# A hybrid decoder trunk: the rows of all experts but the last item are combined on GpSimd, those of the last on TensorE

## The chip, the core and the metric

The kernel runs on one core of a Trainium2 chip. The metric is the device time of one execution in microseconds (us); lower is better. In a core, TensorE (PE) multiplies matrices, VectorE (DVE) and ScalarE (ACT) work elementwise, GpSimd (POOL) works elementwise too and issues the indirect (row by row) transfers, and SyncE (SP) issues transfers. They run at the same time and wait for each other only through semaphores. SBUF is the memory that they work in, PSUM the one that TensorE writes its products to.

## The reference

Two residual layers over 512 tokens of width 1024. Each has a token mixer and then a channel mixer, dense in layer 0 and a mixture of 8 experts in layer 1, of which every token uses two. The trunk ends in an RMS norm. The change concerns only the end of the mixture of experts:

```python
top_logit, top_e = lax.top_k(logits, TOP_K)            # TOP_K = 2
gates = jax.nn.softmax(top_logit, axis=-1)
...                                                    # tokens sorted by expert, in blocks of ROW_BLOCK = 128 rows
def expert_block(args):
    xb, e = args
    return (jax.nn.silu(xb @ w1[e]) * (xb @ w3[e])) @ w2[e]
y_rows = lax.map(expert_block, (x_rows, block_e)).reshape(n_rows, d)
y = jax.ops.segment_sum(y_rows.astype(F32) * row_gate[:, None], row_tok, num_segments=n + 1)[:n]
...
h = h + moe_swiglu(...)
return rms_norm(h, final_norm_g)
```

So every token gets two rows, each from one of its experts and scaled by its gate, added to `h`, and then the final norm.

## The kernel before

All arithmetic is float32. A product on TensorE takes its operands in two parts: `hi`, the operand rounded to a shorter format (a copy on ScalarE), and `lo`, the rest (`raw - hi`, a subtraction on VectorE), and a sum of three products (`mm3`, L582 to L585).

The mixture of experts runs as a loop over work items. An item is an expert's block of 128 rows (L1930 and others, `item_one`), or 128 + up to 32 rows at once in a turned form (`item_turned`). In this run there are eight items; the last is of the form `item_one`. An item takes its expert's weights in 7 chunks of 6 pieces, each 128 x 2048 numbers. A piece is loaded by SyncE, rounded by ScalarE in two halves (`round_ahead`, L1189 and L1191) and its rest is formed by VectorE in two halves (`rest_ahead`, L1774 and L1777: two operands, both in SBUF). The pieces run ahead of TensorE in a ring of six. In a chunk of `item_one`, VectorE does, in this order: pieces 8 and 9, `turned` (L1868), pieces 10 and 11, `hidden` (L1863), pieces 12 and 13, and two additions to `yacc` (L1884). TensorE waits for `turned` before it starts the down product, and for a piece's rest before it uses the piece. At the end of an item VectorE has more to do: rests of two pieces that belong to the next item (for the last item to no one), the rows of the next item (L1879), and the last additions to `yacc`.

`yacc` holds the item's output rows. GpSimd runs the loop beside them (L552 to L565): it clears `yacc` and `yturned`, copies a column of row indices (L545, `gather`), gathers the token rows of the next item to `xg` (L548), waits until the item is complete (`item_out`), stores `yacc` to `y_rows` in HBM (L562, L563), and waits for the store to land. TensorE turns the gathered rows near the end of the item (`turn_rows`, L881), also in the last item, where nobody needs them.

After the loop, GpSimd gathers for each of the four tiles of 128 tokens the first and the second expert's row of every token from `y_rows` (L573, eight gathers of 128 rows of 4 KB), and VectorE adds them, scaled by the gates, to `h` (`combine`, L2018, eight). Between them stands the final norm: a square and sum on ScalarE (L1045), the variance on VectorE (L1342), the root on ScalarE (L1047), its reciprocal (L1347) and the product of `h`, the reciprocal and the gain (L1361). SyncE stores each tile (L487).

The order on each engine is written out by hand: an engine does its instructions in the order of the program, and a wait holds up all behind it.

## Time and profile before

| | |
|---|---|
| time, median of 3 runs | 2075.96 us (2074.44 to 2076.59) |
| the profiled execution | 2074.16 us, of which the profile's span is 2072.5 us |
| PE busy | 1995.7 us, 96% |
| DVE busy | 1576.3 us, 76% |
| ACT busy | 1104.1 us, 53% |
| POOL busy | 89.5 us, 4% |
| DMA | 450.97 MB, mean 218 GB/s |

The busy shares are means over the whole span. By slices of a fortieth of the span, VectorE is at six to nine tenths in the items and TensorE at nine, until the last slice and a half, where TensorE has nothing to do. GpSimd's busy time is in short groups, one at each item's start. Times in the rows are in us from the span's start; a duration in a timeline is that of one instruction or of several merged ones (x2).

### The profile page before, as it was taken

The numbers are of one execution on the slowest core, as the hardware profiler recorded it, in microseconds if no ns is written. First come the engines' busy times: TensorE is split into PE (matmuls) and PEld (weight loads), VectorE is DVE, ScalarE is ACT, GpSimd is POOL, SyncE is SP. The second block draws the span as 40 slices with busy tenths as digits, with TensorE's granted clock in tenths as the row PEclk, the third lists the DMA queues.
The fourth block names the chain that finished last, engine by engine and source line by source line (L and its number), as shares of the span: only waits on it lengthen the run. The fifth ranks groups of instructions, "written<-read, shape, count | busy, mean of one in ns | idle before, by whom it ended". The sixth has DMA issues, their size and how long they took to land.

```text
span 2072.5 us, 34371 instructions
## 1 busy us (share of the span) xinstructions
PE 1995.7 (96%) x12246; PEld 1770.0 (85%) x12247; DVE 1576.3 (76%) x1964; ACT 1104.1 (53%) x1269; POOL 89.5 (4%) x104
## 2 busy tenths in 40 slices
PE   7999999999999999999999999999999999999993
PEld 6889787877778788999999988888999888999882
DVE  6866535344468677888888899998888998888996
ACT  6532423323345423555555577777555776555773
POOL 0000000000000002100100010101000101000101
PEclk9999999999999999999999999999999999999997
DMA  5312723132312215777777699999777999776983
GB/s 195 105 59 92 265 80 119 64 121 63 119 61 92 71 52 170 250 261 259 250 252 260 231 378 368 364 379 340 270 243 244 340 378 325 254 259 235 375 318 144
DMA packets 218811, 450.97 MB, mean 218 GB/s; under 512 B 13088, under 2 KB 64304, under 8 KB 218768
## 3 DMA queue, kind: packets, MB, share of 16 engines
q1 hardware_dynamic: 210416, 421.05, 58.2%
q0 software_dynamic: 8352, 29.33, 3.8%
q8 instruction: 29, 0.48, 0.1%
q14 instruction: 14, 0.11, 0.0%
HBM read 432.50 MB, written 17.84 MB: 217 GB/s over the span
## 4 chain that ended last, share of the span: by engine, by line
PE 83%; DVE 10%; issue 3%; ACT 2%; DMA 1%; DVEq 0%; POOL 0%; ACTq 0%; SPq 0%; POOLq 0%
PE ps L583 17%; PE ps L585 17%; PE ps L584 17%; PE ps L925 12%; PE ps L942 8%; PE ps L927 5%; PE ps L944 3%; DVE w_lo L1777 2%; DVE w_lo L1774 1%; PE ps L652 1%; ACT w_hi L1189 1%; DVE w_lo L1331 1%; PE ps L607 1%; PE ps L846 1%; DVE ex L1356 0%
## 5 line engine op out<-in xcount | busy, mean ns | idle before, releaser
L1774 DVE TENSOR_TENSOR w_lo<-raw,w_hi 128x1024 fp32r<-128x1024 f32 x340 | 414.5, 1219 | 81.9 <-ACT w_hi L1189 79.5
L925 PE MATMUL ps<-xt,w_hi 128*128 128x320 f32 x1792 | 465.3, 347 | 2.2 <-DVE xt L1788 1.9
L927 PE MATMUL ps<-xt,w_lo 128*128 128x160 f32 x1792 | 424.2, 237 | 0.0
L1189 ACT ACTIVATE w_hi<-raw 128x1024 fp32r<-128x1024 f32 x340 | 357.4, 1051 | 112.6 <-PE ps L927 61.2
L1777 DVE TENSOR_TENSOR w_lo<-raw,w_hi 128x1024 fp32r<-128x1024 f32 x340 | 414.1, 1218 | 0.0
L1191 ACT ACTIVATE w_hi<-raw 128x1024 fp32r<-128x1024 f32 x340 | 356.4, 1048 | 0.0
L927 PEld LDWEIGHTS ps<-xt,w_lo 128*128 128x128 f32 x1792 | 343.1, 191 | 0.1
L925 PEld LDWEIGHTS ps<-xt,w_hi 128*128 128x128 f32 x1792 | 337.2, 188 | 2.8 <-issue 2.7
L583 PE MATMUL ps<-act_hi,w_hi 128*128 128x512 f32 x608 | 242.1, 398 | 5.2 <-DVE act_lo L1375 5.2
L585 PE MATMUL ps<-act_hi,w_lo 128*128 128x512 f32 x608 | 239.9, 395 | 0.0
L584 PE MATMUL ps<-act_lo,w_hi 128*128 128x512 f32 x608 | 239.9, 395 | 0.0
L942 PE MATMUL ps<-ht,w_hi 128*128 128x320 f32 x896 | 234.0, 346 | 3.5 <-DVE gated L1897 3.5
L944 PE MATMUL ps<-ht,w_lo 128*128 128x160 f32 x896 | 212.3, 237 | 0.0
L583 PE MATMUL ps<-w_hi,xt 128*128 128x512 f32 x448 | 177.7, 397 | 0.7 <-issue 0.7
L585 PE MATMUL ps<-w_hi,xt 128*128 128x512 f32 x448 | 177.9, 397 | 0.0
L584 PE MATMUL ps<-w_lo,xt 128*128 128x512 f32 x448 | 177.1, 395 | 0.0
L942 PEld LDWEIGHTS ps<-ht,w_hi 128*128 128x128 f32 x896 | 168.1, 188 | 4.4 <-DVE gated L1897 4.2
L944 PEld LDWEIGHTS ps<-ht,w_lo 128*128 128x128 f32 x896 | 171.1, 191 | 0.0
L1696 DVE TENSOR_TENSOR hid_d<-silu_d,ps 128x512 f32<-128x512 f32 x22 | 15.1, 688 | 173.0 <-PE ps L585 173.0
L583 PEld LDWEIGHTS ps<-act_hi,w_hi 128*128 128x128 f32 x608 | 114.4, 188 | 34.3 <-issue 3.9
L585 PEld LDWEIGHTS ps<-act_hi,w_lo 128*128 128x128 f32 x608 | 114.4, 188 | 27.1
L584 PEld LDWEIGHTS ps<-act_lo,w_hi 128*128 128x128 f32 x608 | 114.4, 188 | 26.9 <-issue 0.5
(330 smaller groups left out, 3174.7 us busy)
## 6 DMA issues: line engine op xcount, KB each, us to landing
raw<-in_moe_w_dram SPq DMA_DIRECT2D x672, 512.0 KB, 5.4
raw<-in_w_in_dram SPq DMA_DIRECT2D x19, 1024.0 KB, 5.1
raw<-in_ffn_w_gate_dram SPq DMA_DIRECT2D x11, 1024.0 KB, 5.3
raw<-in_ffn_w_up_dram SPq DMA_DIRECT2D x11, 1024.0 KB, 5.4
raw<-in_ffn_w_down_dram SPq DMA_DIRECT2D x11, 1024.0 KB, 4.9
raw<-in_w_out_dram SPq DMA_DIRECT2D x8, 1024.0 KB, 5.0
y_rows<-mult POOLq DMA_DIRECT2D x1, 8192.0 KB, 29.5
y_rows<-yacc POOLq DMA_DIRECT2D x8, 512.0 KB, 5.5
```

The source lines that it names most:

```text
L583: pe.matmul(o_, lhi, rhi, start=start, stop=False)
L584: pe.matmul(o_, lhi, rlo, start=False, stop=False)
L585: return pe.matmul(o_, llo, rhi, start=False, stop=stop)
L607: last = pe.transpose(ps[:, k, i * P:(i + 1) * P], rows_of(m, i)[:, k * P:(k + 1) * P], idt[:, :])
L925: pe.matmul(pairs_of(ps[:, bank, 0:2 * NW]), hi_[:, k % 4, f * P:(f + 1) * P], xt[:, k, :, 0:NW], start=k == 0, stop=False)
L927: last = pe.matmul(ps[:, bank, NW:2 * NW], lo_[:, k % 4, f * P:(f + 1) * P], xt[:, k, 0, 0:NW], start=False, stop=k == KT - 1)
L942: pe.matmul(pairs_of(ps[:, bank, 0:2 * NW]), hi_[:, f % 2, d * P:(d + 1) * P], ht_n[:, f, :, :], start=f == 0, stop=False)
L944: last = pe.matmul(ps[:, bank, NW:2 * NW], lo_[:, f % 2, d * P:(d + 1) * P], ht_n[:, f, 0, :], start=False, stop=f == 3)
L1189: act.activation(slot_hi[p % 6][:, 0:half], raw6(p)[:, 0:half], ACT.Copy).then_inc(w_hi_half, 1)
L1191: act.activation(slot_hi[p % 6][:, half:PIECE], raw6(p)[:, half:PIECE], ACT.Copy).then_inc(w_hi_done, 1)
L1774: dve.tensor_tensor(slot_lo[p % 6][:, 0:half], raw6(p)[:, 0:half], f32(slot_hi[p % 6][:, 0:half]), ALU.subtract)
L1777: dve.tensor_tensor(slot_lo[p % 6][:, half:PIECE], raw6(p)[:, half:PIECE], f32(slot_hi[p % 6][:, half:PIECE]), ALU.subtract).then_inc(w_lo ...
```

## The change

The last item is taken out of GpSimd's loop. Beside it GpSimd no longer gathers rows for a next item. It gathers the rows of all other items from `y_rows` (the last item's rows are zero there), tile by tile, into `xg`, scales them by the gates (a multiplication by one number for each row) and adds them to `h` (eight of each, 128 x 1024). Then it builds `chosen`, a 0/1 matrix of rows by tokens, from the row indices and a list of the token numbers, and loads the gain of the norm. The last item's rows aren't stored. ScalarE and VectorE split `yacc` into `hi` and `lo` when it is complete, and TensorE multiplies them with `chosen`: 8 products with 512 columns for each tile of tokens, of which four have the 32 rows of the item's second part. VectorE adds the product to `h`, scaled by `g_last`, each token's gate for the last item (seven small instructions ahead of the items). A row that holds no token now has the index 512, that of an added row of zeros in `hn_rows`. TensorE's transposes of `xg` in the last item are as before; they now wait until GpSimd is through, by the two small transfers at its end. A root on ScalarE ahead of the norm loads its table.

```diff
@@ -196,12 +196,16 @@
         w_lo2 = sb("w_lo2", [P, 3, PIECE], F32R)
-        comb = [at(f"comb{i}", [P, D], F32, mix0 + i * 4096) for i in range(8)]
         yacc = sb("yacc", [P, 2, D])
+        xg0 = base[0]
         xg = [sb(f"xg{i}", [P, D]) for i in range(2)]
...
         yturned = sb("yturned", [P, KT, NW])
-        growf = yturned.rearrange("p k n -> p (k n)")[:, 0:D]
+        assert 2 * T <= D
+        chosen = at("chosen", [P, 2, T], F32R, xg0)
+        growf = xg[1]
+        last_hi = [w_his[:, b, 0:D] for b in range(2)]
+        last_lo = [w_los[:, b, 0:D] for b in range(2)]
...
@@ -224,7 +230,7 @@
-        hn_dram = nc.dram_tensor("hn_rows", (T, D), F32, kind="Internal").ap()
+        hn_dram = nc.dram_tensor("hn_rows", (T + 1, D), F32, kind="Internal").ap()
         y_dram = nc.dram_tensor("y_rows", ((MAX_BLOCKS + 1) * P, D), F32, kind="Internal").ap()
@@ -509,6 +524,7 @@
                 .then_inc(y_zeroed, 16)
+            pool.dma_start(hn_dram[T:T + 1, :], mult[0:1].rearrange("p c t -> p (c t)")).then_inc(y_zeroed, 16)
             pool.wait_ge(rows_done, 8)
...
@@ -549,7 +565,7 @@
-            with pool.Fori(0, n_items) as n:
+            with pool.Fori(0, n_items - 1) as n:
                 pool.memset(yacc[:, :, :], 0.0).then_inc(yacc_free, 1)
@@ -564,17 +580,42 @@
-            pool.wait_ge(w_lo_done, n_items * IP + (MOE0 + AHEAD))
+            pool.memset(yacc[:, :, :], 0.0).then_inc(yacc_free, 1)
+            pool.memset(yturned[:, :, :], 0.0).then_inc(yacc_free, 1)
+            block = pool.value_load(items[0:1, bass.ds(n_items + 15, 1)], min_val=0, max_val=MAX_BLOCKS - 1)
+            pool.dma_start(token_at[:, :], token_row.partition_broadcast(P)).then_inc(token_rows, 16)
             for b in range(2):
-                pool.wait_ge(xg_loaded[b], n_items * 16)
+                pool.tensor_copy(colf[:, b:b + 1], idx[:, bass.ds(block + b, 1)]).then_inc(chosen_ready, 1)
+            pool.wait_ge(chosen_ready, 2)
+            pool.wait_ge(token_rows, 16)
+            pool.wait_ge(xt_tr, n_items * 2)
+            pool.wait_ge(gates_final, 1)
             pool.nop(nofuse=True)
...
                 for j in range(2):
-                    pool.indirect_dma_start(comb[2 * i + j][:, :], None, y_dram,
+                    if i:
+                        pool.wait_ge(early_added, 2 * (i - 1) + j + 1)
+                        pool.nop(nofuse=True)
+                    pool.indirect_dma_start(xg[j][:, :], None, y_dram,
                                             bass.IndirectOffsetOnAxis(ap=slots[:, i, j:j + 1], axis=0)) \
                         .then_inc(comb_loaded[2 * i + j], 16)
-                if i == 0:
-                    pool.dma_start(growf[:, :], norm_rows[4].partition_broadcast(P)).then_inc(gain_loaded, 16)
+                for j in range(2):
+                    pool.wait_ge(comb_loaded[2 * i + j], 16)
+                    if j:
+                        pool.wait_ge(early_added, 2 * i + 1)
+                    pool.tensor_scalar(xg[j][:, :], xg[j][:, :], rt[:, 12, 4 * j + i:4 * j + i + 1], None, ALU.mult) \
+                        .then_inc(early_scaled, 1)
+                    pool.wait_ge(early_scaled, 2 * i + j + 1)
+                    pool.tensor_tensor(h[:, i, :], xg[j][:, :], h[:, i, :], ALU.add).then_inc(early_added, 1)
+            pool.wait_ge(early_added, 2 * NT)
+            for b in range(2):
+                pool.tensor_scalar(chosen[:, b, :], token_at[:, :], colf[:, b:b + 1], None, ALU.is_equal) \
+                    .then_inc(chosen_ready, 1)
+            pool.dma_start(growf[:, :], norm_rows[4].partition_broadcast(P)).then_inc(gain_loaded, 16)
+            pool.wait_ge(gain_loaded, 16)
+            pool.wait_ge(chosen_ready, 4)
+            for b in range(2):
+                pool.dma_start(token_at[0:1, b * 8:b * 8 + 8], token_row[:, 0:8]).then_inc(xg_loaded[b], 16)
@@ -1009,6 +1050,26 @@
+            pe.wait_ge(chosen_ready, 4)
+            pe.wait_ge(tail_ready, 1)
+            for i in range(NT):
+                to = slice(i * P, (i + 1) * P)
+                for half in range(2):
+                    s_ = slice(half * 512, (half + 1) * 512)
+                    if i == 0:
+                        pe.wait_ge(last_lo_done, half + 1)
+                    pe.matmul(ps[:, 2 * i + half, :], chosen[:, 0, to], last_hi[0][:, s_], start=True, stop=False)
+                    pe.matmul(ps[:, 2 * i + half, :], chosen[:, 0, to], last_lo[0][:, s_], start=False, stop=False)
+                for half in range(2):
+                    s_ = slice(half * 512, (half + 1) * 512)
+                    if i == 0 and half == 0:
+                        pe.wait_ge(last_lo_done, 3)
+                    pe.matmul(ps[:, 2 * i + half, :], chosen[0:TAIL, 1, to], last_hi[1][0:TAIL, s_],
+                              start=False, stop=False)
+                    last = pe.matmul(ps[:, 2 * i + half, :], chosen[0:TAIL, 1, to], last_lo[1][0:TAIL, s_],
+                                     start=False, stop=True)
+                last.then_inc(spread_done, 1)
+
@@ -1313,6 +1374,12 @@
+            act.wait_ge(tail_ready, 1)
+            for half in range(2):
+                s_ = slice(half * 512, (half + 1) * 512)
+                act.activation(last_hi[0][:, s_], yacc[:, 0, s_], ACT.Copy).then_inc(last_hi_done, 1)
+            act.activation(last_hi[1][0:TAIL, :], yacc[0:TAIL, 1, :], ACT.Copy).then_inc(last_hi_done, 1)
+            act.activation(var[:, 0:1], var[:, 0:1], ACT.Sqrt)
             norm(4)
@@ -1857,6 +1924,15 @@
             link(dve.tensor_tensor(g2, rt[:, 9, 4:8], g1, ALU.mult))
+            starts, last_start, in_last = rt[:, 15, 8:16], rt[:, 15, 16:17], rt[:, 15, 20:24]
+            g_last = rt[:, 12, 16:20]
+            link(dve.scalar_tensor_tensor(starts, blocks, 0.0, first_block, ALU.is_gt, ALU.mult))
+            link(dve.tensor_reduce(last_start, starts, AX.X, ALU.max))
+            link(dve.tensor_scalar(last_start, last_start, float(P), None, ALU.mult))
+            link(dve.tensor_scalar(in_last, rt[:, 16, 0:4], last_start, None, ALU.is_ge))
+            link(dve.tensor_tensor(g_last, g1, g2, ALU.subtract))
+            link(dve.tensor_tensor(g_last, g_last, in_last, ALU.mult))
+            dve.tensor_tensor(g_last, g_last, g2, ALU.add).then_inc(gates_final, 1)
@@ -2013,28 +2089,33 @@
-            def combine(i, j):
-                dve.wait_ge(comb_loaded[2 * i + j], 16)
-                ins = dve.scalar_tensor_tensor(h[:, i, :], comb[2 * i + j][:, :], (g1, g2)[j][:, i:i + 1], h[:, i, :],
-                                               ALU.mult, ALU.add)
-                if j:
-                    ins.then_inc(h_ready, 1)
-                else:
-                    link(ins)
-
-            for i in range(NT + 1):
-                if i < NT:
-                    combine(i, 0)
-                if i:
-                    norm_var(4, i - 1)
-                if i < NT:
-                    combine(i, 1)
-                if i:
-                    norm_row(4, i - 1)
+            dve.wait_ge(item_out, n_items * 4 + 4)
+            dve.sem_inc(tail_ready, 1)
+            for half in range(2):
+                s_ = slice(half * 512, (half + 1) * 512)
+                dve.wait_ge(last_hi_done, half + 1)
+                dve.tensor_tensor(last_lo[0][:, s_], yacc[:, 0, s_], f32(last_hi[0][:, s_]), ALU.subtract) \
+                    .then_inc(last_lo_done, 1)
+            dve.wait_ge(last_hi_done, 3)
+            dve.tensor_tensor(last_lo[1][0:TAIL, :], yacc[0:TAIL, 1, :], f32(last_hi[1][0:TAIL, :]), ALU.subtract) \
+                .then_inc(last_lo_done, 1)
+            dve.wait_ge(early_added, 2 * NT)
+
+            def spread(i):
+                dve.wait_ge(spread_done, i + 1)
+                dve.scalar_tensor_tensor(h[:, i, :], ps[:, 2 * i:2 * i + 2, :].rearrange("p a d -> p (a d)"),
+                                         g_last[:, i:i + 1], h[:, i, :], ALU.mult, ALU.add).then_inc(h_ready, 1)
+
+            spread(0)
+            for i in range(NT):
+                if i < NT - 1:
+                    spread(i + 1)
+                norm_var(4, i)
+                norm_row(4, i)
...
@@ -2095,7 +2176,8 @@
     a.update(norm_rows=norm_rows, params=np.stack(packed), ident=np.eye(P, dtype=np.float32), masks=masks,
-             moe_const=mc, zeros=np.zeros(((MAX_BLOCKS + 1) * P, 1), np.uint32))
+             moe_const=mc, no_token=np.full(((MAX_BLOCKS + 1) * P, 1), T, np.uint32),
+             token_row=np.arange(T, dtype=np.float32)[None, :])
     return {k: a[k] for k in _INS}
```

What GpSimd does from the last item's store on, in the program before (`y_rows` is in HBM, `comb` the eight tiles of gathered rows):

```order
L562 DMA y_rows<-yacc 128x1024
L563 ISA
L563 DMA y_rows<-yacc 32x1024
L564 ISA
L552 REGISTER_ALU
L552 COMPARE_AND_BRANCH
L567 ISA
L569 REGISTER_ALU
L573 DMA comb_87<-y_rows,slots 128x1024
L573 DMA comb_88<-y_rows,slots 128x1024
L577 DMA yturned<-in_norm_rows_dram 128x1024
L573 DMA comb_89<-y_rows,slots 128x1024
```

What it does now behind the loop and the two MEMSETs, while the last item runs, into the first tile (`h` is the residual, `rt` holds the gates):

```order
L586 DMA mcon<-in_token_row_dram 128x512
L588 ISA
L588 COPY colf<-idx 128x1
L588 ISA
L588 COPY colf<-idx 128x1
L591 REGISTER_ALU
L599 DMA xg_88<-y_rows,slots 128x1024
L599 DMA xg_89<-y_rows,slots 128x1024
L606 ISA
L606 TENSOR_SCALAR xg_88<-xg_88,rt 128x1024
L609 TENSOR_TENSOR h<-xg_88,h 128x1024
L606 TENSOR_SCALAR xg_89<-xg_89,rt 128x1024
```

The gathers moved from behind the last item's store to beside the item, and GpSimd has two elementwise instructions for each of them, which read SBUF. VectorE behind the item loop, before, to the first tile's output (`yacc` is the output tile here):

```order
L2018 SCALAR_TENSOR_TENSOR h<-comb_87,rt,h 128x1024
L2018 SCALAR_TENSOR_TENSOR h<-comb_88,rt,h 128x1024
L2018 SCALAR_TENSOR_TENSOR h<-comb_89,rt,h 128x1024
L1342 TENSOR_SCALAR small<-small 128x1
L2018 SCALAR_TENSOR_TENSOR h<-comb_90,rt,h 128x1024
L1347 RECIPROCAL small<-small 128x1
L1361 SCALAR_TENSOR_TENSOR yacc<-h,small,yturned 128x1024
```

And now:

```order
L2092 ISA
L2097 TENSOR_TENSOR w_lo<-yacc,w_hi 128x512 x2
L2100 TENSOR_TENSOR w_lo<-yacc,w_hi 32x1024
L2106 SCALAR_TENSOR_TENSOR h<-ps,rt,h 128x1024 x2
L1409 TENSOR_SCALAR small<-small 128x1
L1414 RECIPROCAL small<-small 128x1
L1428 SCALAR_TENSOR_TENSOR yacc<-h,small,xg_89 128x1024
```

Four of the eight scaled additions are gone from VectorE's end, and three short subtractions stand ahead of them.

## Rows read from the trace of the kernel before

**Rows 1.** The chain that ended last, end of the span (start, us, what).
```profile
2040.87 2.96 DMA y_rows<-yacc
...
2045.02 0.99 POOL comb L573
...
2048.18 7.38 DMA comb<-y_rows,slots
2055.58 1.30 DVE h L2018
```

**Rows 2.** The timeline at the last item's end (start, duration, engine, line).
```profile
2020.59 1.22 DVE L1774 TENSOR_TENSOR w_lo<-raw,w_hi 128x1024 fp32r<-128x1024 f32 x1 [0.67 <-ACT w_hi L1189]
...
2029.76 0.91 PEld L881 LDWEIGHTS ps<-idt,xg 128*128 128x128 f32 x8
...
2037.51 0.39 PE L584 MATMUL ps<-w_lo,ht 128*128 128x512 f32 x1
2037.74 0.39 PE L585 MATMUL ps<-w_hi,ht 128*128 128x512 f32 x1
2038.67 0.68 DVE L1884 TENSOR_TENSOR yacc<-yacc,ps 128x512 f32<-128x512 f32 x1
...
2067.50 0.15 DVE L1342 TENSOR_SCALAR small<-small 128x1 f32<-128x1 f32 x1
...
2068.11 1.28 DVE L1361 SCALAR_TENSOR_TENSOR yacc<-h,small,yturned 128x1024 f32<-128x1024 f32 x1
```

**Rows 3.** Groups of instructions by line: count, busy us, mean ns, then idle before.
```profile
L2018 DVE SCALAR_TENSOR_TENSOR h<-comb,rt,h 128x1024 f32<-128x1024 f32 x8 | 10.3, 1287 | 13.6 <-DMA comb<-y_rows,slots 13.6
...
L1884 DVE TENSOR_TENSOR yacc<-yacc,ps 128x512 f32<-128x512 f32 x56 | 36.1, 680 | 0.0
```

**Rows 4.** ScalarE's timeline at the last item's end.
```profile
2030.22 0.60 ACT L1199 ACTIVATE ht<-ps 128x512 fp32r<-128x512 f32 x1 [3.04 <-PE ps L846]
...
2032.13 1.06 ACT L1189 ACTIVATE w_hi<-raw 128x1024 fp32r<-128x1024 f32 x1
```

**Rows 5.** Stretches: PE, PEld, DVE, ACT, POOL busy (x), PEclk, DMA share, GB/s.
```profile
830.00:831.00 1.00, 1.00 (x7) 1.00 (x6) 1.00 (x2) 0.99 (x2) 0.73 (x1) 0.54 0.00 0
...
834.00:835.00 1.00, 1.00 (x11) 1.00 (x9) 0.00 (x0) 0.50 (x2) 0.00 (x0) 1.00 1.23 57
...
1957.50:1975.00 17.50, 17.50 (x80) 14.22 (x79) 16.54 (x17) 12.91 (x16) 0.00 (x0) 1.00 1.03 395
...
2041.00:2042.00 1.00, 0.00 (x0) 0.00 (x0) 0.00 (x0) 0.00 (x0) 0.39 (x1) 0.91 0.62 258
```

**Rows 6.** GpSimd and VectorE side by side at the start of two items.
```profile
1324.01 1.22 DVE L1777 TENSOR_TENSOR w_lo<-raw,w_hi 128x1024 fp32r<-128x1024 f32 x1
...
1324.20 1.07 POOL L545 COPY col<-idx 128x1 uint32 x1
...
1628.06 1.22 DVE L1774 TENSOR_TENSOR w_lo<-raw,w_hi 128x1024 fp32r<-128x1024 f32 x1
...
1628.43 0.90 POOL L545 COPY col<-idx 32x1 uint32 x1
```

**Rows 7.** One line's instructions: count, duration ns min/median/max.
```profile
L545 POOL COPY col<-idx x16: 182/368/1067, 848.6 to 1930.2; 128x1 uint32 x8, 32x1 uint32 x8
...
L1331 DVE TENSOR_TENSOR w_lo<-raw,w_hi x27: 2266/2285/2466, 24.2 to 776.5; 128x2048 fp32r<-128x2048 f32 x27
```

**Rows 8.** GpSimd and VectorE at the start of the program.
```profile
23.46 1.04 POOL L499 CAST mask<-igate 128x1024 uint8<-128x1024 f32 x1 [7.13 <-DMA igate<-in_masks_dram]
24.18 2.47 DVE L1331 TENSOR_TENSOR w_lo<-raw,w_hi 128x2048 fp32r<-128x2048 f32 x1
```

**Rows 9.** Whom VectorE waited for from 1940 to 2030 us (us, times, longest).
```profile
DVE w_lo L1774 <- ACT w_hi L1189: 3.4, 5, 0.7
DVE ht L1868 <- ACT ht L1199: 1.3, 5, 0.3
```

**Rows 10.** The gathers to `xg`, of all items.
```profile
DMA to landing us min/median/max: 5.3/6.5/8.1
```

More of the change, by code:

```diff
@@ L100, in build @@
 def build(nc, x, w_in, w_out, w_gate, w_up, w_down, w_router, w1, w3, w2, norm_rows, params, ident,
-          masks, moe_const, zeros, out):
+          masks, moe_const, no_token, token_row, out):
     ctx = ExitStack()
@@ L214, in build @@
         mcon = sb("mcon", [P, NMC])
+        token_at = mcon[:, 0:T]
         wr = sb("wr", [P, KT, NE])
@@ L217, in build @@
         col = sb("col", [P, 2], U32)
+        colf = sb("colf", [P, 2])
         slots = sb("slots", [P, NT, 2], U32)
@@ L352, in build @@
         out_rows = sem("out_rows")
+        token_rows = sem("token_rows")
+        chosen_ready = sem("chosen_ready")
+        gates_final = sem("gates_final")
+        early_added = sem("early_added")
+        early_scaled = sem("early_scaled")
+        tail_ready = sem("tail_ready")
+        last_hi_done = sem("last_hi_done")
+        last_lo_done = sem("last_lo_done")
+        spread_done = sem("spread_done")
         out_stored = [sem(f"out_stored{i}") for i in range(2)]
@@ L537, in _ @@
                 pool.wait_ge(hn_stored[i], 32)
-            pool.wait_ge(y_zeroed, 16)
+            pool.wait_ge(y_zeroed, 32)
             pool.wait_ge(items_ready, 1)
@@ L1530, in mixers @@
                         if layer:
-                            dve.wait_ge(y_zeroed, 16)
+                            dve.wait_ge(y_zeroed, 32)
                         dve.wait_ge(ta_ready, 4 * (layer + 1))
```

4 lines of the change are left out of this document (2 added, 2 removed).

## The prediction

> **What bounds the kernel now.** I read the chain that ended last first, from the end back. From the last addition to `yacc`, which ends at 2038.67 + 0.68 = 2039.35 [rows 2], to the span's end at 2072.5 lie 33.15 us in which TensorE does nothing. They begin with the last item's store (2.96 us to landing), the gathers from `y_rows` (issue from 2045.02, the wait for them 7.38), and end in VectorE's additions to `h` and the norm, tile after tile [rows 1]. This is what the change attacks.
>
> Then the item that it puts work beside. In a chunk of 17.5 us TensorE is busy for all of it and VectorE for 16.54 [rows 5]. So TensorE bounds the chunk, and VectorE has hardly any air: from 1940 to 2030 it waited 3.4 us for ScalarE's rounding and 1.3 us for `ht`, 4.7 in all [rows 9]. At the item's end it is VectorE that the chain runs on: its last wait is 0.67 us before 2020.59, and the last addition ends the item nearly a microsecond after TensorE's last product has started at 2037.74 [rows 2]. What VectorE is late by then is added to the end in full.
>
> **The change: the end.** I count from the last addition's end.
> - The loop's end and the semaphores, until ScalarE starts: 0.9. No row shows it for VectorE. GpSimd took 2045.02 - 2043.83 = 1.2 from the store's landing to its first gather [rows 1], the gather's own start included. Bounds 0.3 and 2.
> - ScalarE rounds two halves of 512 columns, 0.60 each, and the 32 rows, 1024 columns, 1.06 [rows 4]. The rest of the last takes VectorE 1.22 (as L1774 [rows 2]). The first two rests lie beside ScalarE. Sum 0.9 + 0.6 + 0.6 + 1.1 + 1.2 = 4.4.
> - The first tile's last four products: they start 0.23 apart [rows 2], 1.1 with the last one's length: 5.5. The first addition, 1.29 (L2018 [rows 3]): 6.8. The second tile's eight products end at 5.5 + 8 x 0.23 = 7.4, so VectorE waits 0.6: 8.7.
> - A tile's norm, from its variance to its output: 2067.50 to 2068.11 + 1.28, 1.89 [rows 2]. Tile 0 is out at 10.6. Tiles 1 and 2 take 1.29 + 1.89 = 3.2 each: 16.9. The last, 1.9: 18.8. From the last output to the span's end it is 2072.5 - 2069.39 = 3.1: 21.9. TensorE needs 1.85 a tile and is hidden behind VectorE from the second on.
> - The eighth gather, the store, half of the scaled additions and the table load in the norm are gone. That leaves a gain of 33.15 - 21.9 = 11.2.
> - TensorE's clock: with nothing to do from 2038.1 on it was granted full speed until about 2041.9 [rows 5], and 1.2 GHz after. The new products start thinly at about 2041.5 and in earnest at 2043.8. Just after the first item's start the grant was half too, in 830 to 831, and full again by 834 with TensorE busy throughout [rows 5]. One such stretch makes a tile's products 1.9 us longer, of which about 1 reaches VectorE: the gain is 10.2. At 1.2 GHz throughout, 28 products of 0.46 end at 17.5, and the addition, two norms and the store follow: 25.7, a gain of 7.4.
>
> **The change: beside the last item.** GpSimd gets 8 scalings and 8 additions of 128 x 1024 and two comparisons of 128 x 512. All read SBUF. The question is whether VectorE pays for them.
> - GpSimd waits for VectorE. Its copy of one column takes 182 ns at best and 1067 at worst [rows 7]. The one at 1324.20 ended at 1325.27, VectorE's subtraction with two inputs in SBUF at 1325.23. The one at 1628.43 ended at 1629.33, VectorE's at 1629.28 [rows 6]. It got its turn when VectorE's instruction was over.
> - VectorE waits for GpSimd. Of 27 rests of a whole piece, median 2285 ns, the longest took 2466 [rows 7]. It is the one that began at 24.18 while GpSimd's cast of 128 x 1024 (23.46 to 24.50) was running [rows 8]. It was held up by 0.18, until 24.36, which is 0.14 before the cast's end.
> - So I take a read on GpSimd and a subtraction of two SBUF inputs on VectorE to exclude each other, for the whole of either but the last 0.14.
>
> The Trainium skill says so as a rule: in SBUF — State Buffer, section "Who interferes with whom", a VectorE instruction with two SBUF inputs contends with a GpSimd instruction that reads SBUF, and the loser is blocked, not slowed. Applied to this kernel it speaks against the change, and both kinds of row agree with it, the second by 0.18 us only.
>
> The price. One read of 128 x 1024 is the cast's 1.04 [rows 8], held 0.90. For the addition, which reads two tensors, no row exists. Bounds: as the cast (held 0.90), or three passes of it (held 2.98). I take two passes, 2.08, held 1.94, since it differs from the cast by one more read. A comparison of half the width is held 0.45. Sum: 8 x 0.90 + 8 x 1.94 + 2 x 0.45 = 23.6 us. Not all of it meets a subtraction. A chunk of VectorE is 12 of these and four instructions of 0.68 with an operand in PSUM [rows 3], and 3 of the 12 are followed by one or two of those: (0.6 + 0.6 + 1.2) / 12 = 0.2 is hidden for each of the 18. That leaves 20.0. VectorE can use up its waits, 4.7 [rows 9]. **VectorE, and with it the item, ends 15.3 us later.** With the bounds: 7.0 and 23.6.
>
> TensorE can be 4 us behind before it is held up, but as VectorE ends the item, this slack gives nothing back.
>
> For the addition the Trainium skill has a price: GPSIMD Engine Reference, section "3.1 Elementwise — side-by-side cycle accounting", gives 4497 ns for 2048 columns. By an estimate from it, 1024 columns take 2.25, and the sum would be 1.4 us more.
>
> The rest. The eight gathers and two broadcasts (some 4.7 MB) come while the DMA engines are at 1.03 [rows 5]. VectorE's rests free the slots of the loads, so these ask for a fifth less while it is held up, and I put this at 0 (bound: 4). The seven small instructions on VectorE ahead of the items, some 1.5, lie before the first item's waits for ScalarE: 0 (bound 1.5). The added row, the index list and its longer wait are long done when needed: 0.
>
> TensorE now waits for GpSimd ahead of L881, 2029.76 before [rows 2], 2045 with the delay. GpSimd's way there: start 1934 after two clears and the token list; a tile takes a gather of 6.5 [rows 10], two scalings and two additions with four turns of VectorE of 1.1, so 6.5 + 6.2 + 4.4 = 17. Four tiles, the comparisons and two transfers end near 2015. It is in time by 30 us.
>
> **Sum.** 2074.16 (profiled execution) - 10.2 + 15.3 = 2079.3. The median is 1.8 above the profiled execution, so 2081.1, which is 5.1 above 2075.96. A change of this kernel's time is told from none at about 0.2%, 4.15 us.
>
> **Rivals.**
> - *GpSimd's work is free.* The two take turns for single accesses, not for whole instructions: 18 delays of 0.18 make 3.2, less than VectorE's 4.7 of waits. For it: 0.18 is all that a row shows in this direction, and VectorE's subtractions in rows 6 keep their 1.22. Against: the copies' ends, to 0.05 us. Then only the end counts: 2075.96 - 10.2 = 2065.8, faster. It decides once a GpSimd instruction costs VectorE less than (10.2 + 4.7) / 18 = 0.8 us. Chance 0.22.
> - *GpSimd is late.* If each of its instructions took some 1.8 us longer (18 x 1.8 = 32), TensorE would stand at L881, and every further microsecond is paid in full. Nothing in the rows speaks for it but that additions are unseen. At 3 us longer each: 2081 + 22 + more blocking, above 2100. Chance 0.04.
> - *The end gains less.* TensorE at 1.2 GHz throughout and a loop's end of 2 us: a gain of 6.3 and 2085. For it: TensorE is nearly idle for 5.6 us ahead of its products, and after 3.8 idle us the grant fell. Chance 0.12.
> - The forecast, chance 0.62. Its own range is from 7.0 - 10.2 to 23.6 - 10.2 about 2076: 2073 to 2089.
>
> **How the numbers follow.** The predicted time is the forecast's, 2081. The range reaches down to the free case, 2066, and up to 2089; a tenth is left out. Faster by over 0.2%: the free case, 0.22. Within 0.2% (2071.8 to 2080.1): a good third of the forecast, additions near the cast's price, and little of the others: 0.27. Slower: 0.51.
>
> **What would show it.** In the profile after: VectorE's subtractions of 1.22 stretched to 2 or 3 us, or gaps ahead of them, wherever GpSimd scales or adds, about 20 us in all, and the last addition to `yacc` at 2054 in place of 2039. GpSimd's additions near 2.1 when nothing delays them and 3.2 with VectorE's turn. Behind the last addition 22 to 24 us to the end. I am wrong if the subtractions stay at 1.22 with GpSimd busy (then the time is 2066), or if GpSimd's additions are near 1 us.

## The result and the profile after

The changed kernel takes 2085.97 us (median of 6 runs, 2085.22 to 2087.05), the kernel before 2075.78 (6 runs, 2074.44 to 2076.59). The ratio is 1.0051, 95% interval 1.0038 to 1.0064: slower by 10.2 us, twice the 5.1 that were forecast, and inside the range of 2066 to 2089. Two medians in the table of the experiments (scalings only; joined, clock held) count one far longer execution each, of 4614.52 and 2389.05 us, which the ratios leave out. The profiled execution took 2087.05, with a span of 2085.4, 12.9 above the span before. That is more than 10.2 because the profiled execution of before lies 1.6 below its median and that of after 1.1 above.

The span is read in three parts, divided at two events that both kernels have. The first is the store of the item before the last (its first row is `y_rows<-yacc`), called the cut from here on. The second is the end of the last addition to `yacc`.

GpSimd's timeline before, then after, at the cut:
```profile
1916.95 0.58 POOL L562 DMA_DIRECT2D y_rows<-yacc  x1 [163.03 <-ACT yacc L1307]
```
```profile
1918.79 0.58 POOL L578 DMA_DIRECT2D y_rows<-yacc  x1 [163.03 <-ACT yacc L1368]
```
VectorE's last `ht` of the last item before, and then its timeline after, from there to the end:
```profile
2031.47 0.68 DVE L1868 TENSOR_TENSOR ht<-ps,ht 128x512 fp32r<-128x512 f32 x1
```
```profile
2048.65 0.68 DVE L1944 TENSOR_TENSOR ht<-ps,ht 128x512 fp32r<-128x512 f32 x1
...
2055.15 0.69 DVE L1960 TENSOR_TENSOR yacc<-yacc,ps 128x512 f32<-128x512 f32 x1 [2.09 <-PE ps L626]
...
2058.26 0.69 DVE L1960 TENSOR_TENSOR yacc<-yacc,ps 128x512 f32<-128x512 f32 x1 [0.15 <-PE ps L626]
...
2060.53 1.29 DVE L2097 TENSOR_TENSOR w_lo<-yacc,w_hi 128x512 fp32r<-128x512 f32 x2 [1.57 <-ACT w_hi L1380]
...
2065.46 1.28 DVE L2106 SCALAR_TENSOR_TENSOR h<-ps,rt,h 128x1024 f32<-128x1024 f32 x1 [2.25 <-PE ps L1069]
...
2069.37 1.28 DVE L2106 SCALAR_TENSOR_TENSOR h<-ps,rt,h 128x1024 f32<-128x1024 f32 x1 [2.63 <-PE ps L1069]
...
2073.38 1.28 DVE L2106 SCALAR_TENSOR_TENSOR h<-ps,rt,h 128x1024 f32<-128x1024 f32 x1 [0.91 <-PE ps L1069]
...
2077.39 1.28 DVE L2106 SCALAR_TENSOR_TENSOR h<-ps,rt,h 128x1024 f32<-128x1024 f32 x1 [0.91 <-PE ps L1069]
...
2081.01 1.28 DVE L1428 SCALAR_TENSOR_TENSOR yacc<-h,small,xg 128x1024 f32<-128x1024 f32 x1
```
- Ahead of the cut: 1918.79 - 1916.95 = 1.8 later.
- The item, from there to the last addition's end (2058.95): 140.2 us, where it was 2039.35 [rows 2] - 1916.95 = 122.4. So 17.8 longer.
- The end: 2085.4 - 2058.95 = 26.5 in place of 33.15. So 6.7 shorter.

1.8 + 17.8 - 6.7 = 12.9, the whole difference of the spans.

The last item after, by lines (1925 to 2056 us; count, busy us, mean ns, idle before):
```profile
L1841 DVE TENSOR_TENSOR w_lo<-raw,w_hi 128x1024 fp32r<-128x1024 f32 x40 | 68.5, 1713 | 1.7 <-ACT w_hi L1250 1.7
L1844 DVE TENSOR_TENSOR w_lo<-raw,w_hi 128x1024 fp32r<-128x1024 f32 x40 | 48.7, 1217 | 0.0
L606 POOL TENSOR_SCALAR xg<-xg,rt 128x1024 f32<-128x1024 f32 x8 | 38.4, 4799 | 10.8 <-DMA xg<-y_rows,slots 10.2 <-POOL h L609 0.7
L609 POOL TENSOR_TENSOR h<-xg,h 128x1024 f32<-128x1024 f32 x8 | 21.9, 2738 | 0.7
L612 POOL TENSOR_SCALAR chosen<-mcon,colf 128x512 fp32r<-128x512 f32 x2 | 6.9, 3478 | 0.1
```
Half of VectorE's subtractions keep 1.22 us. The other line's mean is 1.71: (1713 - 1220) x 40 = 19.7 us more. Single ones show where. GpSimd and VectorE together, 1955 to 1962:
```profile
1955.11 3.35 POOL L609 TENSOR_TENSOR h<-xg,h 128x1024 f32<-128x1024 f32 x1
1956.10 3.44 DVE L1841 TENSOR_TENSOR w_lo<-raw,w_hi 128x1024 fp32r<-128x1024 f32 x1
1958.62 4.68 POOL L606 TENSOR_SCALAR xg<-xg,rt 128x1024 f32<-128x1024 f32 x1 [0.17 <-POOL h L609]
1959.46 1.21 DVE L1844 TENSOR_TENSOR w_lo<-raw,w_hi 128x1024 fp32r<-128x1024 f32 x1
...
1961.19 1.46 DVE L1841 TENSOR_TENSOR w_lo<-raw,w_hi 128x1024 fp32r<-128x1024 f32 x1
```
GpSimd's addition seems to get its turn when the subtraction that started at 1954.96 ended, at 1956.18. It ran to 1958.46, and the next subtraction took 3.44 - 1.22 = 2.2 us longer. The subtraction beside the scaling, at 1961.19, took 0.24 longer. All sixteen stretched subtractions of the item are of these kinds: eight of 2.2, seven of 0.23 to 0.32 (the first of the eight scalings stretched none), and one of 0.4 at the comparisons, 19.8 us in all.

The granted clock in three stretches (columns as in rows 5):
```profile
2048.80:2055.70 6.90, 6.14 (x15) 4.79 (x16) 4.81 (x6) 3.09 (x4) 0.00 (x0) 0.51 0.00 0
2055.70:2058.20 2.50, 2.46 (x11) 1.69 (x9) 2.41 (x3) 0.00 (x0) 0.00 (x0) 1.00 0.00 0
...
2062.50:2078.00 15.50, 14.19 (x29) 8.08 (x28) 8.19 (x11) 4.60 (x10) 0.00 (x0) 0.50 0.13 52
```
A grant of 0.50 is 1.2 GHz. TensorE had it from 2062.5 until its last product, though it was busy for 14.19 of these 15.5 us. A tile's eight products took 4.0 us (2077.39 - 2073.38 in the additions), and VectorE, with some 3.1 us of work a tile, waited for them: 6.7 us in 4 waits.

The first of the three stretches lies in the item's last down product. TensorE's first instruction of it, after and then in the run with the clock held (below), with the wait for `ht` ahead of it:
```profile
2049.56 0.79 PE L624 MATMUL ps<-w_hi,ht 128*128 128x512 f32 x1 [2.18 <-DVE ht L1944]
```
```profile
2048.72 0.49 PE L624 MATMUL ps<-w_hi,ht 128*128 128x512 f32 x1 [2.25 <-DVE ht L1946]
```
Before, TensorE did not wait there: it was busy without a break from the cut to the last `ht`.

### The profile page after: what moved, and what is told of

The parts are those of the page before. It is cut to its first block, busy times and chain, and to the rows that moved or that the text cites. A ratio compares the mean times of both kernels' runs of the same rounds, so it can differ in the third digit from the quotient of the medians.

```text
span 2085.4 us, 34457 instructions
## 1 busy us (share of the span) xinstructions
PE 2020.2 (97%) x12278; PEld 1784.0 (86%) x12279; DVE 1595.0 (76%) x1970; ACT 1106.5 (53%) x1273; POOL 166.9 (8%) x122
## 4 chain that ended last, share of the span: by engine, by line
PE 83%; DVE 10%; issue 3%; ACT 3%; DMA 0%; DVEq 0%; ACTq 0%; SPq 0%
PE ps L624 17%; PE ps L626 17%; PE ps L625 17%; PE ps L966 12%; PE ps L983 8%; PE ps L968 5%; PE ps L985 3%; DVE w_lo L1844 2%; DVE w_lo L1841 2%; PE ps L693 1%; ACT w_hi L1250 1%; DVE ex L1423 1%; ACT w_hi L1252 1%; DVE w_lo L1398 1%; PE ps L887 0%
## 5 line engine op out<-in xcount | busy, mean ns | idle before, releaser
L1841 DVE TENSOR_TENSOR w_lo<-raw,w_hi 128x1024 fp32r<-128x1024 f32 x340 | 435.0, 1279 | 79.1 <-ACT w_hi L1250 76.9
L1844 DVE TENSOR_TENSOR w_lo<-raw,w_hi 128x1024 fp32r<-128x1024 f32 x340 | 414.8, 1220 | 0.0
```

The lines of the kernel that those rows point to most:

```text
L1841: dve.tensor_tensor(slot_lo[p % 6][:, 0:half], raw6(p)[:, 0:half], f32(slot_hi[p % 6][:, 0:half]), ALU.subtract)
L1844: dve.tensor_tensor(slot_lo[p % 6][:, half:PIECE], raw6(p)[:, half:PIECE], f32(slot_hi[p % 6][:, half:PIECE]), ALU.subtract).then_inc(w_lo ...
```

## The experiments

The columns item and end are of one profiled execution each: the item from the cut to the last addition's end, the end from there to the span's end. Ratios are to the kernel before on the same chip. Its median was 2074.11 us on the chip of gathers only, scalings only, additions only and additions by DMA, 2074.39 on that of changed again, clock held, gates late and gathered late, and 2075.55 on that of the other four.

| run | median us | ratio, 95% interval | item | end |
|---|---|---|---|---|
| before | 2075.78 | | 122.4 | 33.15 |
| changed | 2085.97 | 1.0051 (1.0038 to 1.0064) | 140.2 | 26.5 |
| gathers only | 2068.19 | 0.9969 (0.9957 to 0.9981) | 122.4 | 26.5 |
| scalings only | 2069.30 | 0.9978 (0.9968 to 0.9987) | 122.4 | 26.5 |
| additions only | 2081.23 | 1.0023 (1.0012 to 1.0035) | 133.6 | 26.4 |
| additions by DMA | 2089.22 | 1.0069 (1.0055 to 1.0083) | 139.7 | 26.5 |
| changed, again | 2087.28 | 1.0064 (1.0050 to 1.0078) | 138.5 | 26.5 |
| clock held | 2079.59 | 1.0032 (1.0021 to 1.0042) | 138.5 | 21.8 |
| gates late | 2085.24 | 1.0058 (1.0044 to 1.0072) | 140.2 | 26.5 |
| gathered late | 2071.34 | 0.9986 (0.9977 to 0.9995) | 122.4 | 29.5 |
| two scalings | 2084.14 | 1.0049 (1.0034 to 1.0063) | 134.8 | 26.5 |
| late, clock held | 2070.84 | 0.9979 (0.9970 to 0.9987) | 122.4 | 29.5 |
| joined by DMA | 2070.63 | 0.9978 (0.9969 to 0.9988) | 122.4 | 29.0 |
| joined, clock held | 2071.30 | 0.9980 (0.9971 to 0.9988) | 122.4 | 29.0 |

The cut lay between 1915.8 and 1922.1 us in these executions, and it differs for the same kernel too (1918.79 and 1921.55), so medians alone do not tell 2 us here. The columns item and end do. From VectorE's first subtraction behind the small operations for the gates, at the start of the first item (837.69 in the changed kernel), to the cut all fourteen executions took 1081.0 to 1081.1 us. So what differs between them ahead of the cut arises ahead of that subtraction.

**Gathers only.**
```diff
-                    pool.tensor_scalar(xg[j][:, :], xg[j][:, :], ...gate..., None, ALU.mult)
-                    pool.tensor_tensor(h[:, i, :], xg[j][:, :], h[:, i, :], ALU.add).then_inc(early_added, 1)
+                    pool.sem_inc(early_added, 1)
```


> Left out of the computation: the rows of the earlier blocks are gathered during the last item as in the changed kernel, but neither scaled nor added to h. Theory A (GpSimd's elementwise work on SBUF holds up VectorE's two-input subtractions: each add stretched one of them by 2.21 us and each scale one by 0.24, 19.7 us in all, and the waits that this gives TensorE cost about 2 more through half-clock stretches): the subtractions of the last item are back at 1.22 to 1.25 us, its last addition ends near 2038 to 2041 of the span instead of 2058.95, and the time is 2063 to 2068. Rival B (it is the gathers: 4 MB of DMA beside the weights, and GpSimd's descriptor writing): most of the loss stays, time 2080 or more, and subtractions stay near 1.7 us mean.

The two lines of subtractions in the last item (the stretched one, L1841 above, is L1838 here and L1839 with the scalings only), and then those of the scalings-only kernel:
```profile
L1838 DVE TENSOR_TENSOR w_lo<-raw,w_hi 128x1024 fp32r<-128x1024 f32 x40 | 48.6, 1216 | 2.6 <-ACT w_hi L1247 2.4
L1841 DVE TENSOR_TENSOR w_lo<-raw,w_hi 128x1024 fp32r<-128x1024 f32 x40 | 49.0, 1226 | 2.3 <-ACT w_hi L1249 2.2
```
```profile
L1842 DVE TENSOR_TENSOR w_lo<-raw,w_hi 128x1024 fp32r<-128x1024 f32 x41 | 50.2, 1225 | 0.0
L1839 DVE TENSOR_TENSOR w_lo<-raw,w_hi 128x1024 fp32r<-128x1024 f32 x40 | 48.6, 1216 | 4.4 <-ACT w_hi L1248 4.4
...
L606 POOL TENSOR_SCALAR xg<-xg,rt 128x1024 f32<-128x1024 f32 x8 | 35.5, 4438 | 15.5 <-DMA xg<-y_rows,slots 14.9 <-POOL xg L606 0.7
```
The item is back at 122.4 to a tenth. The gathers beside it cost nothing, and all of the 17.8 us comes with GpSimd's elementwise work.

**Scalings only** (the `tensor_tensor` line left out) **and additions only** (the `tensor_scalar` line left out).

> Left out of the computation: the eight adds of the gathered, scaled rows into h; the eight scales stay. Theory A (only the adds are expensive: an instruction of GpSimd with two inputs in SBUF holds VectorE's two-input subtraction off for its whole 2.2 us, one with one input for a quarter of a us): 2 us above the run with gathers only, 2065 to 2070. Rival C (every GpSimd instruction costs VectorE its own duration; a scale lasts 4.7 us in the profile, an add 2.7): the scales cost more than the adds, at least 15 us, time 2079 or more. Prediction's held cost of a scale (0.90 us each, 7.2 in all) would give 2071 to 2074.

> Left out of the computation: the eight scales by the gates; the unscaled rows are added to h. Theory A: the eight stretches of 2.2 us (17.7 us) stay, time 2081 to 2085, one to four us under the changed kernel. Rival C (cost by GpSimd's duration): 2071 to 2076. The two runs with one part alone should add up: (scale only minus gathers only) plus (add only minus gathers only) = changed kernel minus gathers only, within 3 us, if the costs are independent.

The scalings alone cost the item nothing. The additions alone make it 11.2 longer, with 15.7 us of stretches; the other 4.5 are made up in VectorE's waits. Together they cost 17.8 (16.1 in the execution of changed, again), 6.6 more than the parts. Of these, 4.1 are stretches (19.8 in place of 15.7), and 2.4 come behind the last `ht`. The additions' median of 2081.23 is just inside the expected 2081 to 2085, but three of its seven executions took 2075.8 to 2077.7. By time the parts make 1.1 + 13.0 = 14.1 of some 16.5 us (the changed kernel at 1.0051 of this chip's 2074.11), within the 3 that were allowed; by the item they do not add up. How a scaling can be free shows beside VectorE (scalings only):
```profile
1949.34 5.56 POOL L606 TENSOR_SCALAR xg<-xg,rt 128x1024 f32<-128x1024 f32 x1 [0.17 <-POOL xg L606]
1949.82 1.21 DVE L1839 TENSOR_TENSOR w_lo<-raw,w_hi 128x1024 fp32r<-128x1024 f32 x1
1950.96 1.22 DVE L1842 TENSOR_TENSOR w_lo<-raw,w_hi 128x1024 fp32r<-128x1024 f32 x1
1952.34 0.69 DVE L1942 TENSOR_TENSOR ht<-ps,ht 128x512 fp32r<-128x512 f32 x1 [0.17 <-ACT ht L1258]
```
It lasts through two subtractions that keep their 1.22 us, and ends 2.6 us after the start of the instruction with an operand in PSUM. The shortest scaling here took 2.85, so I take it to have got its turn there.

**Two scalings**: a second `tensor_scalar` of the same tile in place of the addition.

> Left out of the computation: the eight adds; in the place of each stands a second scale of the same tile (128x1024, one input in SBUF and one scalar for each partition), so that GpSimd has as many elementwise instructions as in the changed kernel and is busy longer. Theory A (only an instruction of GpSimd with two inputs in SBUF takes VectorE's time): the last item lasts 122.4 to 124 us from the store ahead of it to its last addition, as with gathers only, and the ratio to the kernel before is 0.997 to 0.998. Rival C (GpSimd's elementwise work costs by its number or duration): 16 scales take over what the adds took, item 133 us or more, time 2079 or more. A late GpSimd (its sequence then ends later, by 8 times about 2 us) can add at the end only if it ends behind 2041, which costs at most 5 us and shows as a wait for the 0/1 matrices.

This went against the theory: 134.8 us, not 122.4 to 124. GpSimd and VectorE, then the wait of TensorE:
```profile
1956.94 4.79 POOL L606 TENSOR_SCALAR xg<-xg,rt 128x1024 f32<-128x1024 f32 x1 [0.17 <-POOL xg L609]
1957.87 1.22 DVE L1842 TENSOR_TENSOR w_lo<-raw,w_hi 128x1024 fp32r<-128x1024 f32 x1
1959.01 2.06 DVE L1845 TENSOR_TENSOR w_lo<-raw,w_hi 128x1024 fp32r<-128x1024 f32 x1
1960.99 0.68 DVE L1940 TENSOR_TENSOR gated<-gated,ps 128x512 f32<-128x512 f32 x1
```
```profile
2044.47 2.96 PE L923 MATMUL ps<-idt,xg 128*128 128x128 f32 x16 [8.73 <-DMA mcon<-in_token_row_dram]
```
A scaling that gets its turn between two subtractions (this one ends 2.7 us after the boundary at 1959.01) stops the next for 0.84 us, and then goes on beside it. Fourteen of the sixteen stretched one, by 0.3 to 0.84; with 0.4 at the comparisons the stretches make 10.4. The last `ht` came 6.0 us later than in the kernel before (counted from the cut). The other 6.4 come behind it: GpSimd's sequence ended at 2043.8, and TensorE stood for its token 8.7 us. In the changed kernel it ended at 2041.0 and TensorE came at 2045.7. So one-input work is cheaper but not free, and the margin of GpSimd's path was some 3 us. Rival C's item and time came true, its reason only in part: the eight second scalings were busy for 32.2 us where the additions took 21.9, and yet the subtractions were stretched by 10.4 us in place of 19.8.

**Additions by DMA.**
```diff
-                    pool.tensor_tensor(h[:, i, :], xg[j][:, :], h[:, i, :], ALU.add).then_inc(early_added, 1)
+                    pool.dma_start(h[:, i, :], xg[j][:, :], accum_op=ALU.add).then_inc(early_added, 16)
```


> The whole computation: GpSimd still scales the gathered rows, but each 128x1024 tile is added to h by a DMA that accumulates in place of GpSimd's addition. Theory A: VectorE's subtractions lose 2 us instead of 19.9, the last item ends about 18 us earlier, time 2065 to 2070 if GpSimd's chain ends before the item does (near 2038 of the span). Rival D (an accumulating DMA is slow or its issue is: GpSimd's chain has eight more landings in it, about 3 to 7 us each by the gathers' landings of 5.3 to 8.1, and ends after the item): TensorE waits for the 0/1 matrices at the end, each us behind 2041 costs one, time 2075 to 2095.

The subtractions lost only 1.1 us, as theory A has it. The time was lost elsewhere. Lines of the item, then GpSimd's queue in 1940 to 2040 with gathers only and with the additions by DMA:
```profile
L1842 DVE TENSOR_TENSOR w_lo<-raw,w_hi 128x1024 fp32r<-128x1024 f32 x41 | 50.0, 1219 | 11.3 <-ACT w_hi L1251 11.0
L1845 DVE TENSOR_TENSOR w_lo<-raw,w_hi 128x1024 fp32r<-128x1024 f32 x40 | 49.9, 1248 | 12.0 <-ACT w_hi L1253 11.8
```
```profile
q0 software_dynamic: 1360, 4.72, 11.6%
```
```profile
q0 software_dynamic: 2304, 8.39, 31.3%
```
VectorE now waits for weights, through ScalarE's rounding. The queue's share of the 100 us rose by 31.3 - 11.6 = 19.7%, so the eight accumulations of 512 KB occupied some 19.7 us of all 16 engines, 2.5 each (2.6 if the gain's transfer, which lies only in the first of the two windows, is taken off). These engines were full already (1.03 [rows 5]). Neither theory had named this; rival D's time was right, its reason was not: behind the last `ht` the item took no longer than before, so TensorE did not wait for GpSimd.

**Changed, again; clock held; gates late.**

> The changed kernel unaltered, on the same chip as the next three, so that they can be set against it: ratio to the kernel before of 1.005, as in the result.

```diff
             pe.wait_ge(chosen_ready, 4)
+            spin(ps[:, 3, 0:P], 24)
             pe.wait_ge(tail_ready, 1)
...
                     if i == 0 and half == 0:
+                        spin(ps[:, 7, 0:P], 6)
                         pe.wait_ge(last_lo_done, 3)
```


> The whole computation, plus 24 transposes of the identity on TensorE between the last item's last product and the 0/1 products, and 6 more ahead of the second block's. Theory E (the end gained 6.7 us instead of 10.2 because TensorE came to it after a gap of 3.2 us, was granted 1.2 GHz from 2062.5 on, and so took 4.0 us for each tile, for which VectorE waited 6.7 us in 4 waits): the granted clock stays at 1.00 from 2060 to 2075, a tile's eight products take about 2.1 us, VectorE's waits for them fall to about 1.5 us, and the time is 3 to 5 us under the changed kernel's. Rival F (VectorE's own work of some 3.2 us for each tile and the waits between VectorE and ScalarE set the end, the clock hides nothing more): under 1.5 us. Rival G (the transposes delay the products): slower.

With the clock held (columns as in rows 5):
```profile
2055.70:2068.00 12.30, 11.26 (x51) 7.12 (x49) 7.84 (x10) 6.10 (x12) 0.00 (x0) 1.00 0.05 21
```
The end takes 21.8 us in place of 26.5: 4.7 us are the clock's, shown. The medians differ by 7.7, more than the 3 to 5 expected. In the profiled executions, 9.1 apart in span, another 4.3 lie ahead of the cut (1917.24 against 1921.55), which the edit does not touch; whether the medians' other 3.0 are of this kind is not shown.

Gates late: the seven small operations stand behind the splits.

> The whole computation, with the seven small VectorE operations for the gates of the last block moved from ahead of the first item to the place behind the last item's splits, where VectorE waits 2.1 us for TensorE. Theory H (they put the whole chain of the items off by 1.7 to 1.85 us, which nothing takes up, because the items are bound by VectorE and TensorE): 1.3 to 1.9 us under the changed kernel's. Rival I (a wait in the first item takes them up, as the prediction had it at nothing): within 0.5 us.

VectorE's stretch from the start of `g2` (the multiplication just ahead of the seven) to the first subtraction behind them was 3.59 us (834.10 to 837.69) in the changed kernel and is 2.15 here; in the kernel before it was 2.33. So they cost 1.3 to 1.4, and as the way from that subtraction to the cut is the same in all, the cut comes later by as much. The medians differ by 2.0 with overlapping intervals, which alone would settle nothing.

**Gathered late.** GpSimd only gathers, into buffers of raw weights that are free; VectorE does the rest behind the item, in a new order there, with the seven small operations ahead of the splits.
```diff
+        early = [[raw6((4, 5, 0, 1)[i])[:, j * D:(j + 1) * D] for j in range(2)] for i in range(NT)]
...
+            for i in range(NT):
+                pool.wait_ge(w_lo_done, n_items * IP + (MOE0 + i - 1))
+                for j in range(2):
+                    pool.indirect_dma_start(early[i][j][:, :], None, y_dram, ...slots[:, i, j:j + 1]...)
...
+            def earlier(i, j):
+                link(dve.scalar_tensor_tensor(h[:, i, :], early[i][j], (g1, g2)[j][:, i:i + 1], h[:, i, :],
+                                              ALU.mult, ALU.add))
```


> The whole computation, in another division: the earlier blocks' rows are gathered at the end of the last item, each tile's two as soon as a buffer of raw weights comes free (the four come free 16, 14, 11 and 9 us before the item's last addition), and VectorE scales and adds them after the item by the kernel before's fused operation, so GpSimd does no elementwise work on them; the comparisons stand at the item's start, the seven small operations where VectorE waits for the first split. Theory A (what cost the changed kernel its gain is GpSimd's additions beside VectorE's subtractions): the last item ends where it did with gathers only, 18 us earlier than in the changed kernel; the end takes 26 to 29 us in place of 26.45, as eight operations of 1.2 us fill VectorE's waits and 3 us more; the time is 2067 to 2071 on the chip where the kernel before takes 2074 to 2076, so both are beaten, by 0.1 to 0.4%. Rival J (the gathers' issue, 4 to 5 us each on GpSimd while VectorE has its two-input subtractions, or the late landings set the end): VectorE waits for gathered rows, time 2072 to 2080.

It beats both kernels, by 0.14% against the one before (interval 0.05% to 0.23%); item and end together take 151.9 us in place of 155.6. The gathers took 0.94 to 1.97 us to issue and were never waited for. The end, 29.5, is half a microsecond over the expected bounds.

> The whole computation: the division with the gathers at the item's end and VectorE's eight fused operations behind it, plus the 24 and 6 transposes that hold TensorE's clock. Theory K (here VectorE is the bound of the end: it is busy for 25.4 of the 29.5 us, with no wait for TensorE behind its first product): the granted clock is 1.00 where it was 0.50, and the time moves by less than 1 us. Rival E (a slow clock costs 4.7 us wherever the 0/1 products stand): 3 to 5 us faster.

The grant in 2040 to 2050, without and with the transposes:
```profile
2040.00:2050.00 10.00, 6.69 (x14) 4.08 (x15) 8.66 (x15) 4.73 (x7) 0.00 (x0) 0.65 0.02 9
```
```profile
2040.00:2050.00 10.00, 8.27 (x37) 5.20 (x35) 9.50 (x16) 4.93 (x8) 0.00 (x0) 1.00 0.01 2
```
The end stays at 29.5, as theory K has it: here VectorE is the bound, and TensorE's clock is worth nothing.

**Joined by DMA**: `early[i][1]` is scaled by GpSimd and `dma_start(early[i][0], early[i][1], accum_op=ALU.add)` adds it, then one fused operation of VectorE a tile; and the same with the transposes.

> The whole computation: as with the gathers at the item's end, but of each tile's two gathered rows GpSimd scales the second by the ratio of the gates and an accumulating DMA adds it to the first, so VectorE has four fused operations behind the item in place of eight. The weights' transfers are over by then, so the accumulations meet no full queue. Expected: item 122.4 us, GpSimd's four scales 2.7 to 4.7 us each and four landings of about 8, the last by 2058 of the span; VectorE sheds 4.8 us but then meets TensorE's 4.0 us for each tile, so the end takes 26.5 us as with the changed kernel's, in place of 29.5; time 3 us under the division with eight, ratio to the kernel before 0.997. Rival: a join lands late, VectorE waits for it, no gain.

> The whole computation: as the run before, plus the transposes that hold the clock. Now both bounds are lowered: TensorE's tile takes 2.2 us, VectorE's 3.9. Expected: the end takes 22 to 24.5 us, the time is 5 to 7 us under the division with eight fused operations and 3 to 4 under the run with joins alone; ratio to the kernel before 0.995 to 0.9965. Rival: joins land late (each us behind VectorE's need is lost) and it stays at 0.997 or more.

Both ends are 29.0, where 26.5 and 22 to 24.5 were expected: 4.8 us of VectorE's work are gone and only 0.5 came back. VectorE in the kernel gathered late, then in the one joined and held:
```profile
2041.74 0.23 DVE L2081 TENSOR_SCALAR rt<-rt 128x4 f32<-128x4 f32 x1
...
2043.68 1.21 DVE L2091 TENSOR_TENSOR w_lo<-yacc,w_hi 32x1024 fp32r<-32x1024 f32 x1
```
```profile
2041.35 1.33 DVE L2102 TENSOR_SCALAR rt<-rt 128x4 f32<-128x4 f32 x1
...
2044.39 2.13 DVE L2112 TENSOR_TENSOR w_lo<-yacc,w_hi 32x1024 fp32r<-32x1024 f32 x1
...
2048.77 1.28 DVE L2122 SCALAR_TENSOR_TENSOR h<-ps,rt,h 128x1024 f32<-128x1024 f32 x1 [1.05 <-PE ps L1081]
```
```profile
2050.00:2060.00 10.00, 10.00 (x21) 5.77 (x20) 8.61 (x12) 3.86 (x8) 2.46 (x2) 0.50 0.58 138
```
GpSimd's scalings now stand beside the splits. Counted from the last addition's end, the splits are through 7.2 us later in place of 4.7: the two rows above lose 1.1 and 0.9, and the first of the small operations 0.5 (0.66 us in place of 0.17). So TensorE started its last products later, and VectorE waited 2.2 us for it in two waits, where it had waited for none. In the held kernel TensorE was granted 0.50 from 2050 on in spite of the transposes, so that run does not show what a full clock would give there. All four late versions lie within 0.1% of each other. Which of them is the best is open.

## Why the prediction was right, point by point

The sign and the range were right, and the main term nearly exact. Part of that is luck: its two prices erred in opposite directions, and the change came out at twice the forecast, because three smaller terms all erred towards too fast.

- **Beside the item, the sum: right.** Counted from the cut, VectorE's last `ht` came at 129.9 us (2048.65 - 1918.79); in the kernel before, at 114.5 (2031.47 - 1916.95). That is 15.3 later, as forecast. In the other three executions with the same work beside the item it was 14.9, 16.1 and 16.5 (changed again, clock held, gates late), so the agreement to a tenth is chance. The stretches made 19.8 (19.3 to 20.9 in those three), forecast 20.0. The difference to 15.3 is 4.5, forecast 4.7 as waits used up; VectorE's idle time from the cut to that `ht` fell from 7.7 to 3.9.
- **Its two prices: one too high, one too low.** "Held 0.90" for a scaling: in these four executions 4 of 32 scalings stretched no subtraction, 18 stretched one by 0.23 to 0.32 and 10 by 0.83. "Held 1.94" for an addition: 2.2 in 28 of 32. In the profiled execution of the result this makes 8 x 0.24 + 8 x 2.2 + 0.4 = 19.9 in place of 8 x 0.90 + 8 x 1.94 + 0.9 - 3.6 = 20.0. The sum held because the errors cancelled.
- **Exclusion "for the whole of either": half wrong.** It holds for the addition. A scaling of 2.6 to 2.9 us excludes VectorE for no more than 0.84 of them. The Trainium skill (SBUF — State Buffer, "Who interferes with whom") calls the contention for the shared ports an exclusive lock. The trace agrees with that for the additions (2.2 us) and not for the scalings (0 to 0.84), and the measurement decides. The addition's price from GPSIMD Engine Reference in the Trainium skill, "3.1 Elementwise — side-by-side cycle accounting", an estimate of 2.25, agrees with the 2.2 measured.
- **"As VectorE ends the item, this slack gives nothing back": the step that failed inside the item.** It lets the item end with VectorE's delay and no more. Behind the last `ht` the item took 2.4 us longer than before (140.2 - 129.9 against 122.4 - 114.5). TensorE had stood 2.2 us for the delayed `ht` ahead of 2049.56, was granted 0.51 from 2048.8 to 2055.7, and VectorE waited 2.1 for it. With changed again and with gates late this part was 1.3. With the clock held it was 0: there TensorE had stood as long (2.25 us), but its products behind started 0.23 apart, at full clock. So the half clock makes this part, and not the pause by itself. Why the grant fell there in three executions and not in the fourth is open.
- **The end: the term that was mis-sized.** Forecast a gain of 10.2, with the half clock in one stretch at the start and full clock after it; measured 6.7. It came the other way round: full clock to 2062.5, and 0.50 from there to the last product. The variant worked out beside it, 1.2 GHz throughout, had 25.7 us and a gain of 7.4. The other steps hold: with full clock the end is 21.8, forecast 21.9, and ScalarE started 0.9 behind the last addition, as estimated.
- **"The seven small instructions: 0 (bound 1.5)": wrong,** 1.3 to 1.4. The wait that I took for cover is one for ScalarE that comes after the first two pieces and moves with them. Before, then after:
```profile
842.88 1.23 DVE L1774 TENSOR_TENSOR w_lo<-raw,w_hi 128x1024 fp32r<-128x1024 f32 x1 [1.49 <-ACT w_hi L1189]
```
```profile
844.60 1.23 DVE L1841 TENSOR_TENSOR w_lo<-raw,w_hi 128x1024 fp32r<-128x1024 f32 x1 [1.49 <-ACT w_hi L1250]
```
- **The gathers at 0: right.** GpSimd's path "in time by 30 us": wrong. It ended at 2041 in place of 2015. The first two gathers took 9.9 us to issue, and a scaling waited up to 4 us for its turn (mean 4.8 with the wait). Some 3 us were left.
- In the profiled executions: 1.8 + 17.8 - 6.7 = 12.9, forecast 15.3 - 10.2 = 5.1. The misses are 1.8 ahead of the item, 2.4 in it and 3.5 at the end. Of the first, 1.3 is the small operations and the rest differs between executions anyway.

The rival "free" fell with the 2.2 us of the additions; for the scalings alone it was true. The rival "the end gains less" was right on the clock. Its gain of 6.3 and its 2085 are nearer to the measured 6.7 and 2086 than the forecast's 10.2 and 2081 are, but it reached them partly by a loop's end of 2 us, which took 0.9.

## What to carry to other kernels

An engine that looks idle is not free: ask which of its instructions read what memory in two streams, and beside which of the busy engine's. In a stretch where VectorE has 16.5 of 17.5 us and DMA 1.03, the same additions were paid for whether GpSimd did them (17.8 us) or accumulating DMAs (17.3), while the gathers alone, and with them the scalings alone, cost nothing there. The same rows gathered late and added behind the item cost 3.0 us. Where a path ends in products behind a pause, work out the sum at the half clock first, and take the gain of holding the clock only where TensorE is what the next engine waits for.

## What the runs showed of the hardware

- GpSimd's addition of two SBUF tiles (128x1024) mostly stopped VectorE's two-input subtraction for 2.2 us. Its scaling by a per-partition scalar did so for 0.83 or 0.84 where its turn, counted back 2.6 us from its end (an estimate from these runs), fell between two subtractions. Where the turn fell at an instruction with a PSUM operand or in a pause, it was 0 to 0.68, mostly under 0.33.
- An accumulating DMA of 512 KB within SBUF occupied the 16 engines for some 2.5 us; a gather of as much, by the same queue (4.72 MB in 11.6 us), 1.3. Both are shares of the queue's packets.
- Next to GpSimd's scaling even a VectorE instruction of 4 columns took 1.33 us in place of 0.23.
- The second gather of the last item took 4.3 to 4.8 us to issue at about 1940, the first 1.0 or, in two executions, 4.8 and 5.1. Later ones took 0.9 to 2.0, but for two of 4.1 and 5.4 with the gathers only. Why is open.
